# Head norms with sums, roots and spreads laid out over four quarters of the array and of a bank

## The reference

```
def rms_norm(x, gain):
    xf = x.astype(jnp.float32)
    y = xf * lax.rsqrt(jnp.mean(xf * xf, axis=-1, keepdims=True) + NORM_EPS)
    return (y * gain.astype(jnp.float32)).astype(x.dtype)
```

## Time and profile before

| What | Value |
|---|---|
| median of 3 runs | 4768.86 us (4768.56 to 4769.66) |
| the profiled execution, own time | 4769.85 us |
| its span, first to last instruction | 4768.1 us |
| TensorE busy | 4498.3 us, 94% of the span |
| ScalarE, VectorE, GpSimd busy | 1461.5, 2004.3, 1842.5 us |
| mean granted clock of TensorE | 0.972 |
| products of sums (line 816), busy | 81.9 us in 168 passes |
| products of spreads (line 830), busy | 85.6 us in 152 passes |

### The profile page before, as it was taken

How to read it: one execution, slowest core, us unless ns; L and a number is a source line. 1 busy time by engine, 2 the same in 40 slices (tenths; PEclk the granted TensorE clock), 3 DMA queues, 4 the chain that set the end, 5 groups by cost and what they waited for, 6 DMA issues and landing times. The chain is left out here.

```text
span 4768.1 us, 51289 instructions
## 1 busy us (share of the span) xinstructions
PE 4498.3 (94%) x19930; PEld 3524.0 (74%) x19930; DVE 2004.3 (42%) x4177; ACT 1461.5 (31%) x2188; POOL 1842.5 (39%) x828
## 2 busy tenths in 40 slices
PE   7778899999999999999999979899999998788999
PEld 6557578888888888887887836588878874365887
DVE  8463369933332333333441252444144135645440
ACT  2153323344443111112222235432232232344221
POOL 3015144466665444444444401244444431032443
PEclk9789999999999999999999989999999999999999
DMA  3213134455555655654222201222222221021222
GB/s 139 45 50 111 44 102 135 139 166 177 172 183 190 196 186 184 197 184 148 93 97 94 97 16 36 67 91 95 97 89 97 95 85 51 18 76 49 97 94 83
DMA packets 220707, 520.43 MB, mean 109 GB/s; under 512 B 25649, under 2 KB 91569, under 8 KB 217521
## 3 DMA queue, kind: packets, MB, share of 16 engines
q1 hardware_dynamic: 135984, 450.03, 28.9%
q10 hardware_dynamic: 84480, 67.12, 4.3%
HBM read 445.77 MB, written 71.30 MB: 108 GB/s over the span
## 5 line engine op out<-in xcount | busy, mean ns | idle before, releaser
L196 POOL TENSOR_TENSOR ring_rounded<-ring,highs_rounded 128x1024 fp32r<-128x1024 f32 x687 | 1681.2, 2449 | 2644.2 <-ACT highs_rounded L190 2644.2
L442 PE MATMUL bank<-arena_rounded,ring_rounded 128*128 128x512 f32 (+1 forms) x4488 | 1778.9, 396 | 85.1 <-DVE hT_rounded L460 41.5
L444 PE MATMUL bank<-arena_rounded,highs_rounded 128*128 128x512 f32 (+1 forms) x4488 | 1757.9, 392 | 0.0
L190 ACT ACTIVATE highs_rounded<-ring 128x1024 fp32r<-128x1024 f32 x687 | 728.1, 1061 | 2039.1 <-PE bank L444 1598.5
L443 PE MATMUL bank<-hT_rounded,highs_rounded 128*128 128x512 f32 x3128 | 1221.6, 391 | 0.0
L442 PEld LDWEIGHTS bank<-arena_rounded,ring_rounded 128*128 128x128 f32 x4488 | 853.8, 190 | 271.4 <-issue 82.5
L444 PEld LDWEIGHTS bank<-arena_rounded,highs_rounded 128*128 128x128 f32 x4488 | 850.6, 190 | 193.9
L443 PE MATMUL bank<-arena_rounded,highs_rounded 128*128 128x512 f32 (+1 forms) x2112 | 824.3, 390 | 0.0
L443 PEld LDWEIGHTS bank<-hT_rounded,highs_rounded 128*128 128x128 f32 x3128 | 592.6, 189 | 125.3 <-issue 0.2
L443 PEld LDWEIGHTS bank<-arena_rounded,highs_rounded 128*128 128x128 f32 x2112 | 402.4, 191 | 86.4
L1526 DVE TENSOR_TENSOR arena<-qT,arena 128x512 f32<-128x512 f32 x64 | 149.9, 2342 | 363.6 <-ACT qT L1491 363.0
(11 more groups left out here) (351 smaller groups left out, 4172.8 us busy)
## 6 DMA issues: line engine op xcount, KB each, us to landing
ring<-pages_in SPq DMA_DIRECT2D x687, 512.0 KB, 3.4
act_table<-arena SPq DMA_DIRECT2D x128, 256.0 KB, 4.0
gate_table<-qT SPq DMA_DIRECT2D x16, 2048.0 KB, 7.2
arena<-act_table ACTq DMA_DIRECT2D x128, 256.0 KB, 3.9
arena<-gate_table ACTq DMA_DIRECT2D x32, 1024.0 KB, 8.0
arena<-mem_in SPq DMA_DIRECT2D x3, 1024.0 KB, 5.1
arena<-spread_in SPq DMA_DIRECT2D x5, 512.0 KB, 4.4
xT<-x_in SPq DMA_DIRECT2D x8, 256.0 KB, 6.2
```

What stands on the lines that cost most here:

```text
L190: nc.scalar.activation(f32r(page_high(p)), slot(p), ACT.Copy).then_inc(masked_pages.sem, 1)
L196: nc.gpsimd.tensor_tensor(f32r(slot(p)), slot(p), part_of(page_high(p)), ALU.subtract).then_inc(split_pages.sem, 1)
L442: low_last = nc.tensor.matmul(out, f32r(w_low), f32r(x_high), start=start, stop=False)
L444: return low_last, nc.tensor.matmul(out, f32r(w_high), f32r(x_high), start=False, stop=stop)
```

## The change

The 32 rows become four times 32.

- The sums of unit u go to quarter u % 4 of the bank's rows, which is also a quarter of the array's columns: `bank[0][32*(u%4) : 32*(u%4)+32]`, at rows 2*(u//4) and the next of that quarter. The product is 128 x 32 as before. The first product of each quarter starts its accumulation (`start=(u < 4 and c == 0)`).
- The roots are taken on 128 rows instead of 32, with the same operations. The three memsets that cleared 96 rows of `small` are gone, since every row is now written.
- The spread of unit u is a product of 32 rows: `spread[quarter(u), u, :]` with `rms[quarter(u)]`. It occupies the quarter u % 4 of the array's rows and all its columns. Banks, waits and buffers are as before.
- The matrix `spread` is laid out on the host to match; its size and its transfer are unchanged.

```diff
-            rms = small[0:32, :]
-            mean = newton[0:32, 0, :]
+            rms = small[:]
+            mean = newton[:, 0, :]
+
+            def quarter(u):
+                return slice(32 * (u % 4), 32 * (u % 4) + 32)
...
-                    nc.scalar.activation(rms, bank[0][0:32, :], ACT.Ln, bias=gcol("eps")[0:32],
+                    nc.scalar.activation(rms, bank[0][:], ACT.Ln, bias=gcol("eps"),
...
-                            last = nc.tensor.matmul(bank[0][0:32, 0:long[u]],
-                                                    mats[:, window[0], window[1] + 30 - 2 * u:window[1] + 62 - 2 * u],
-                                                    sq[:, u % 2, c, 0:long[u]], start=(u == 0 and c == 0),
-                                                    stop=(u == count - 1 and c == len(chunks) - 1),
+                            at = window[1] + 30 - 2 * (u // 4)
+                            last = nc.tensor.matmul(bank[0][quarter(u), 0:long[u]], mats[:, window[0], at:at + 32],
+                                                    sq[:, u % 2, c, 0:long[u]], start=(u < 4 and c == 0),
+                                                    stop=(u >= count - 4 and c == len(chunks) - 1),
                                                     skip_group_check=True)
...
-                            nc.tensor.matmul(bank[1 + u % 3][:, 0:long[u]], spread[:, u, :], small[:, 0:long[u]], start=True,
-                                             stop=True).then_inc(full.sem, 1)
+                            nc.tensor.matmul(bank[1 + u % 3][:, 0:long[u]], spread[quarter(u), u, :],
+                                             rms[quarter(u), 0:long[u]], start=True, stop=True).then_inc(full.sem, 1)
...
-                    for r in range(32, P, 32):
-                        nc.vector.memset(small[r:r + 32, :], 0.0)
...
-                    nc.vector.tensor_scalar(mean, bank[0][0:32, :], 1.0 / width, EPS, ALU.mult, ALU.add)
+                    nc.vector.tensor_scalar(mean, bank[0][:], 1.0 / width, EPS, ALU.mult, ALU.add)
...
-                    b = newton[0:32, 1, :]
+                    b = newton[:, 1, :]
...
-    for r in range(32):
-        spread[r, r // 2, r % 2 * 64:r % 2 * 64 + 64] = 1
+    for u in range(16):
+        for j in range(2):
+            spread[32 * (u % 4) + 2 * (u // 4) + j, u, 64 * j:64 * j + 64] = 1
```

## The result

The changed kernel is slower: 4806.52 us median of 4 runs (4803.52 to 4819.12) against 4768.71 (4768.51 to 4769.66), a ratio of 1.0084 with a 95% interval of 1.0068 to 1.0100. The prediction was 4764 us with a range of 4755 to 4777; the measured time lies above the range, and above the time of every rival. The nearest, "products of 32 rows don't hold the clock up", stood at 4795 us and 7%.

The account below looks back on a forecast made before the run. TensorE, 94% busy, was taken to bound the kernel, with the head-norm calls as closed blocks whose savings count fully. -6.8 - 7.6 + 2.1 + 7 = -5.3 us against 4769.85 or 4768.86 gave 4764 us, range 4755 to 4777.

Parts of the forecast that it names:

- products of 32 rows don't hold the clock up: Rival, 7%: turns of calls 3, 6 and 7 take 4.0 instead of 2.46 us at 1.2 GHz; +31, 4795 us.
- Do quarters overlap: Sums and spreads: products on different array quarters run at once at full speed, as halves did in the trace.
- The sums, -6.8: Eight calls' sums: with overlap only the buffer loop bounds; 1.32 instead of 1.71 us a unit at 1.2 GHz; -6.8 us.
- The spreads, -7.6: Eight calls' spreads: three products out at once, 0.95 us a unit at 1.2 GHz, 0.66 at 2.4 GHz; -7.6 us.
- The turns, +2.1: Calls 3, 6, 7: two shape switches a turn, hidden under VectorE at 2.4 GHz, not at 1.2 GHz; +2.1 us.
- What costs nothing: Roots on 128 partitions and dropped memsets: 0 us, at worst 2.4 us for the root operations.
- What the clock takes back, +7: Sums, spreads and turns: TensorE's new gaps prolong the 1.2 GHz level, 3 us longer in half of 15 stretches; +7 us.
- The two other rivals on the clock: Clock keeps its course despite gaps: 4756.5 us, 15%; or sums stay at 1.2 GHz to their end: 4777 us, 15%.
- allowance of 3 us: Attention stages behind the calls change clock level often and shift in time: 3 us either way.
- Only the columns don't overlap: Rival, 8%: the sums' 6.8 us gain and half of the clock's toll fall away; -2, 4767 us.

Follow-up runs that it names:

- first experiment: The changed kernel with sums still in four column quarters, but each spread again a product of all 128 rows: 4755.01 us, ratio 0.9971 to the kernel before.
- four square buffers: Sums in column quarters and whole 128-row spreads, with four square buffers instead of two in calls with units of one chunk: 4744.51 us, ratio 0.9941 to the kernel before.
- column halves: The kernel before with each spread made as two products of all 128 rows by 64 columns: 4767.88 us, ratio 1.0003.
- 32-row kernel: The kernel before with each spread a product of rows 0 to 31 only, all in one quarter, without overlap: 4838.12 us, ratio 1.0141.

## Why the prediction was wrong, point by point

- **Do quarters overlap: right.** Row quarters ran at full speed beside each other in threes (six passes in 2.08 us), column quarters in twos and, with four buffers, in threes and fours.
- **The sums, -6.8: right in kind.** The sums alone won 7.9 us (first experiment), in the changed kernel 4.9. The loop of two buffers was named as the next bound; the four square buffers show it.
- **The spreads, -7.6: the mechanism was there, the term was not.** The waits of VectorE shrank as described, but 0.95 us a unit at 1.2 GHz is all there is when the clock never rises. (The terms given for the loop of a bank add up to 2.74 us, not 2.85; it measured 218.94 - 216.06 = 2.88.) Without turns 3.7 us were left.
- **The turns, +2.1: the price of the switch was right** (0.35 us for two at 2.4 GHz; at 1.2 GHz 4.00 us a turn against 4.0). Only its cover failed: it was reckoned at 2.4 GHz, and every turn of the three calls ran at the other level, but for the last 0.3 us of TensorE's work in call 3.
- **What costs nothing: right.** The root operations on 128 partitions take 0.69 us instead of 0.68, and the memsets are not missed.
- **What the clock takes back, +7: this is the step that failed.** It made the low level last longer by the gaps alone. But the clock stayed low through 21.20 us without a gap, and through 13.90 us of the same products one after the other. What mattered was which products ran. In place of +7 stand 34 us in the turning calls and 8 us outside the calls, which is no term of the sum at all except as an allowance of 3 us. The reading behind it was weak as well: of the two stretches with gaps the first holds products of 64 rows (line 1104), so it could not part gaps from few rows.
- **The two other rivals on the clock fall.** It did not keep its course, and the sums did not stay at 1.2 GHz to their end. For the latter the prediction said that the 15% idle of the loop lies between rows 4 and rows 10; it does not, since 5.83 of 6.60 us in rows 10 is 12% idle. The clock rose all the same, after TensorE had been busy 4.70 of 4.90 us.
- **The slower rival had the right mechanism, place and price.** 20 turns at 1.54 us more was its working, 31 us; the turning calls' spreads grew by 34.2 us. Its total of 4795 us was still 11.5 us too low, 8.3 of them outside the calls. I gave it 7% because products of 32 columns had lifted the clock in the trace of before. That was an inference from one side of the array to the other: the row said something about columns, and none of the rows shown was a long stretch of products with few rows. For the same reason the two half-array rows proved the overlap and said nothing on the clock; the first of them lies at its low level.
- **"Only the columns don't overlap" falls.** Four passes on column quarters took 2.43 us at 1.2 GHz, and sixteen 6.03. The Trainium skill (TensorE: Matmul & The Clock Gate, Part 3, "The mechanism") lets weight loads overlap running products only for another row group. These passes do not agree with it. The same part of the Trainium skill gives 3.07 times the speed for four products of 32 rows. The trace agrees that they run at once (six passes in 2.08 us, 5.1 us one after the other), but at the low clock, little of that reaches the kernel.

## What to carry to other kernels

An overlap that is gained by cutting products into row tiles must be weighed at the clock that those products leave behind: here two or three at once at 1.2 GHz did hardly better than one at a time with the clock rising (3.7 us in five calls), and any phase that cannot overlap pays in full. Column tiles won the same overlap without that price. And when one of two equal bounds is lifted (TensorE in the sums), look at once for the other (the two buffers): buffers alone and quarters alone won 0.6 and 7.9 us of sums, together 27.

## What the runs showed of the hardware

- Products of 32 rows ran 13.90 us without a gap at a granted clock of 0.50; products of 96 or 128 rows saw it go to 1.00 after 5.1 us in the same place; products of 128 rows on 32 or 64 columns had it at 1.00 too (208.60 to 212.30 us of the changed kernel, 2775.00 to 2785.50 of the column halves). With 64 rows it rose in calls 5 to 8 while they followed one another, in call 1 only at their end and in call 2 not. The rows left out in the 32-row kernel held zeros, so it isn't the values.
- A whole-array product in every other place didn't help: turns of one 32-row or 64-row product and one of 128 rows stayed at 0.50 (21.20 us of call 3 of the changed kernel without a gap; 25.95 of 26.00 us with 64 rows, from 2772.6 us on).
- A switch between tile shapes costs TensorE, by estimate, 0.18 us at 2.4 GHz (a turn of 2.06 us less the 1.71 of four passes, halved; column halves) and 0.3 us at 1.2 GHz (a turn of 4.00 us less four passes of 0.85, halved; 32 rows).
